# A twelfth weight slot laid over memory that the expert stage doesn't use

## The reference, cut to what matters

```
for layer in range(4):
    mixed = attention | hgrn2 | short_conv (x)          # 8, 10, 8 weight units of 2 MB
    x = layer_norm(alpha * x + mixed)
    logits = x @ w_group, x @ w_expert                  # group, then two experts in it
    h = silu(x @ w_gate[e]) * (x @ w_up[e]) * gate[e]   # e = 0..31, width 256
    x = layer_norm(alpha * x + sum_e h[e] @ w_down[e])
```

## Time and profile before

| what | us |
|---|---|
| median of 3 runs (1506.69 to 1510.03) | 1508.38 |
| the profiled execution | 1506.55 |
| its span, first to last instruction | 1504.4 |
| TensorE busy in it | 1342.5 |
| VectorE, ScalarE, GpSimd busy | 316.8, 312.0, 65.7 |
| bytes read from HBM | 478.22 MB |

### The profile page before, as it was taken

How to read it: one execution, slowest core, us unless ns; L and a number is a source line. 1 busy time by engine, 2 the same in 40 slices (tenths; PEclk the granted TensorE clock), 3 DMA queues, 4 the chain that set the end, 5 groups by cost and what they waited for, 6 DMA issues and landing times.

```text
span 1504.4 us, 18506 instructions
## 1 busy us (share of the span) xinstructions
PE 1342.5 (89%) x7798; PEld 760.4 (51%) x7798; DVE 316.8 (21%) x878; ACT 312.0 (21%) x765; POOL 65.7 (4%) x106
## 2 busy tenths in 40 slices
PE   8999988878999999888779999888789999888775
PEld 7866633332564776333327865332328675533321
DVE  0243311012100843101002133110021161301103
ACT  0242312112221422221112002211111251221110
POOL 2200000000000520000000000000001000000000
PEclk9999999999999999999999999999999999999998
DMA  9756499999733118999998936999997355699995
GB/s 322 290 196 248 162 426 430 426 428 425 301 133 146 58 30 366 415 426 429 426 429 337 388 121 219 431 425 430 426 426 323 113 224 223 251 429 426 428 425 221
DMA packets 35765, 480.60 MB, mean 319 GB/s; under 512 B 4304, under 2 KB 4624, under 8 KB 6368
## 3 DMA queue, kind: packets, MB, share of 16 engines
q1 hardware_dynamic: 34416, 476.79, 76.6%
q0 software_dynamic: 1120, 2.09, 0.7%
q10 hardware_dynamic: 144, 0.48, 0.1%
HBM read 478.22 MB, written 1.05 MB: 319 GB/s over the span
## 4 chain that ended last, share of the span: by engine, by line
PE 68%; DMA 23%; DVE 3%; ACT 3%; issue 1%; SPq 1%; POOL 0%; DVEq 0%; POOLq 0%
DMA ring<-in_units 17%; PE psum L742 15%; PE psum L1017 9%; PE psum L756 9%; PE psum L780 7%; PE psum L993 6%; DMA work<-in_units 5%; PE psum L1047 5%; PE psum L1055 5%; ACT work L1151 2%; PE psum L764 1%; PE psum L707 1%; PE psum L1109 1%; PE psum L820 1%; DVE work L1732 1%
## 5 line engine op out<-in xcount | busy, mean ns | idle before, releaser
L742 PE MATMUL psum<-xT,ring 128*128 128x256 f32 x1024 | 222.4, 379 | 1.4 <-DMA ring<-in_units 1.0
L742 PEld LDWEIGHTS psum<-xT,ring 128*128 128x128 f32 x1024 | 194.2, 190 | 28.8 <-DMA ring<-in_units 1.4
L1055 PE MATMUL psum<-work 128*128 128x512 f32 x256 | 128.7, 629 | 42.9 <-DVE work L1732 22.8
L1017 PE MATMUL psum<-ring,work 128*32 128x512 f32 x1200 | 143.2, 611 | 23.3 <-DMA ring<-in_units 23.3
L993 PE MATMUL psum<-work,x 128*128 128x128 f32 x1024 | 131.4, 283 | 35.1 <-ACT work L1151 35.0
L993 PEld LDWEIGHTS psum<-work,x 128*128 128x128 f32 x1024 | 120.9, 194 | 71.3 <-issue 68.0
L756 PE MATMUL psum<-ring,xT 128*128 128x512 f32 x320 | 138.6, 593 | 0.4 <-ACT xT L1151 0.4
L1151 ACT ACTIVATE work<-psum,affine_t 128x128 f32<-128x128 f32 x256 | 96.2, 456 | 123.9 <-PE psum L993 123.9
L1017 PE MATMUL psum<-work 128*32 128x512 f32 x848 | 104.2, 627 | 14.2 <-DMA work<-in_units 14.2
L1727 DVE TENSOR_TENSOR work<-work,psum 128x256 f32<-128x256 f32 x32 | 13.5, 421 | 484.9 <-ACT work L1318 484.9
L780 PE MATMUL psum<-ring,work 128*128 128x512 f32 x256 | 112.1, 593 | 0.9 <-DVE work L1406 0.9
(11 more groups left out here) (214 smaller groups left out, 1084.4 us busy)
## 6 DMA issues: line engine op xcount, KB each, us to landing
ring<-in_units SPq DMA_DIRECT2D x138, 2048.0 KB, 27.1
work<-in_units SPq DMA_DIRECT2D x83, 2048.0 KB, 26.3
ring<-in_units SPq DMA_DIRECT2D x6, 1024.0 KB, 45.8
ring<-in_units SPq DMA_DIRECT2D x4, 512.0 KB, 10.1
work<-in_units SPq DMA_DIRECT2D x2, 1024.0 KB, 45.0
x<-in_x SPq DMA_DIRECT2D x2, 512.0 KB, 4.1
out<-x SPq DMA_DIRECT2D x2, 512.0 KB, 2.7
work<-in_tables SPq DMA_DIRECT2D x1, 640.0 KB, 30.5
```

The costliest lines, as they stand in the source:

```text
L742: last = nc.tensor.matmul(bank(key, T, s * T), w[:, 2 * m + s, k, :], xT[:, k, :], start=(k == 0), stop=(k == KD - 1))
L1017: last = nc.tensor.matmul(psum[rows, 0, :].rearrange("p (t f) -> p t f", t=2), xw[:, k, rows], w[:, e, kk], start=(k == 0), stop=(k == KD ...
L1055: last = nc.tensor.matmul(psum[:, 4 + NH * c + h, :], hT[:, FC + c, :], y_sb[:, h * HB:(h + 1) * HB], start=False, stop=last_quad, skip_gr ...
```

## The change

The kernel gets a twelfth slot, `last`. It is laid over four things that are not read while the experts run: `xT` (2048 columns), the tables that only mixers, residual and rank use (`tri`, `ones`, `strict`, `alpha`, `causal`; 896 columns), the router weights (288 columns), and the first 864 columns of `work`. They become parts of one buffer, `memory`. The expert stage's own tiles (`scratch`) are packed into 4096 columns behind it; Silu's output goes straight into `h_sb`, and some tiles share places with `y_sb`.

The 48 expert units go through a cycle of 12. In each layer unit 11 is the first in slot `last`; it is loaded in two halves: the one over `xT` when the residual is through (`residual_made`), the other when the rank matmuls are. The down matmuls of unit 11 wait for both. The mixers wait for the reloaded tables ahead of their first use: the cumulative sum of the attention, the lower bounds of HGRN2, the residual of the convolution. Unit 47 uses the slot last. As the slot overwrites the tables and the router weights, SP loads the tables again in layers 1 to 3, behind the mixer's sixth unit and a wait for unit 47, and POOL loads the router weights after unit 47 of the layer before instead of after its logits. With 48 divisible by 12 the cycle ends where it began, so that the mixers' units find other ring slots: in layers 1 and 2 units 0 to 5 follow expert units 36, 37, 38, 39, 45, 46 (before: 42 to 47), in layer 3 units 40 to 44 and 46 (before: 37 to 41 and 43). The affine of the last normalisation, in e0, follows unit 42 (before: 39). `keep_busy` reads the identity four times over instead of 512 columns of tables.

```diff
-SLOTS = RING + EARLY
+SLOTS = RING + EARLY + 1
...
-                 2: [e1, e2, e3, e4] + r[2:] + [r[0], e0, r[1]]}[KINDS[l]]
+                 2: [e1, e2, e3, e4] + r[2:] + [r[0], e0, r[1]]}[KINDS[l]] + [last]
...
-EARLY_AT = 4688
+MIXER_TABLES = CONST_AT["iota"][0]
+SHARED = KD * T + MIXER_TABLES + KD * (NG + NE)
+MOE_SCRATCH = UNIT - SHARED
+EARLY_AT = 4960
...
-        const = sb("const", [P, CONST.shape[1]])
-        work = sb("work", [P, EARLY_AT + EARLY * UNIT])
+        const = sb("const", [P, CONST.shape[1] - MIXER_TABLES])
+        memory = sb("memory", [P, SHARED + EARLY_AT + EARLY * UNIT])
+        work = memory[:, SHARED:]
...
+        xT = region(memory, 0, [KD, T])
+        w_router = region(memory, KD * T + MIXER_TABLES, [KD, NG + NE])
...
+            if n == SLOTS - 1:
+                return memory[:, 0:UNIT]
...
-                    if KINDS[l] == 1 and m == RING - 1:
+                    if l and m == RING - 1:
 
                         sp.wait_ge(*moe_used(l - 1, NQ * QU - 1))
-                        sp.dma_start(tables, a["tables"]).then_inc(spans_in, 16)
+                        sp.dma_start(mixer_tables, a["const"][:, 0:MIXER_TABLES]).then_inc(tables_in, 16)
+                        if KINDS[l] == 1:
+                            sp.dma_start(tables, a["tables"]).then_inc(spans_in, 16)
...
+                if s == SLOTS - 1:
+                    sp.wait_ge(residual_made, l + 1)
+                    sp.dma_start(slot("moe", l, v)[:, 0:KD * T], a["units"][MOE_AT[l] + v][:, 0:KD * T]).then_inc(soon_in, 16)
+                    sp.wait_ge(*filled(("rank", l)))
+                    sp.dma_start(slot("moe", l, v)[:, KD * T:], a["units"][MOE_AT[l] + v][:, KD * T:]).then_inc(unit_in[s], 16)
...
-            sp.dma_start(const[:, first_const:], a["const"][:, first_const:]).then_inc(const_in, 16)
+            sp.dma_start(const[:], a["const"][:, MIXER_TABLES:]).then_inc(const_in, 16)
...
-                    pool.wait_ge(*filled(("logits", l - 1)))
+                    pool.wait_ge(*moe_used(l - 1, NQ * QU - 1))
                 pool.dma_start(w_router[:, :, 0:NG], ...)
...
-                    nc.tensor.matmul(psum[:, bank_no, :], ident, const[:, 0:HB], start=True, stop=True)
+                    nc.tensor.matmul(psum[:, bank_no, :], ident, ident.unsqueeze(1).to_broadcast([P, HB // P, P]), start=True, stop=True)
...
+                pe.wait_ge(tables_in, 16 * (l + 1))
...
+                    if sems is first and n % NQ * QU + GU + h == SLOTS - 1:
+                        pe.wait_ge(soon_in, 16 * (n // NQ + 1))
...
-                    residual([c])
+                    last = residual([c])
+                last.then_inc(residual_made, 1)
...
-                nc.scalar.activation(silu_g, psum[:, 0, 0:ED], ACT.Silu).then_inc(sems["silu_ready"], 1)
+                nc.scalar.activation(h_sb, psum[:, 0, 0:ED], ACT.Silu).then_inc(sems["silu_ready"], 1)
```

More of the change, by code:

```diff
@@ L70, in slot_plan @@
     order = list(range(RING))
-    e0, e1, e2, e3, e4 = range(RING, SLOTS)
+    e0, e1, e2, e3, e4, last = range(RING, SLOTS)
     def put(unit, slot):
@@ L287, in build @@
         x = sb("x", [P, TC, D])
-        xT = sb("xT", [P, KD, T])
         affine_t = sb("affine_t", [P, 2 * DEPTH, 2, KD])
-        const = sb("const", [P, CONST.shape[1]])
-        work = sb("work", [P, EARLY_AT + EARLY * UNIT])
+        const = sb("const", [P, CONST.shape[1] - MIXER_TABLES])
+        memory = sb("memory", [P, SHARED + EARLY_AT + EARLY * UNIT])
+        work = memory[:, SHARED:]
         extra = work[:, O_AT + TC * D:]
         small = sb("small", [P, 512])
-        w_router = sb("w_router", [P, KD, NG + NE])
         b_router = sb("b_router", [P, DEPTH, NG + NE])
         taps = sb("taps", [P, CW, KD])
-        most = sb("most", [P, DEPTH], I32)
         psum = ctx.enter_context(nc.psum_tensor("psum", [P, 8, HB], F32))
+        mixer_tables = memory[:, KD * T:KD * T + MIXER_TABLES]
         def table(name):
-            return const[:, CONST_AT[name][0]:CONST_AT[name][1]]
+            first, end = CONST_AT[name]
+            return mixer_tables[:, first:end] if end <= MIXER_TABLES else const[:, first - MIXER_TABLES:end - MIXER_TABLES]
         ident, ones, tri, strict = (table(n) for n in ("ident", "ones", "tri", "strict"))
@@ L325, in build @@
         lf_z = region(work, O_AT + 576, [TC, HEADS])
-        wf = region(work, 4544, [KD, HEADS])
-        bf = region(work, 4672, [HEADS])
+        wf = region(work, EARLY_AT - KD * HEADS, [KD, HEADS])
+        bf = region(small, 176, [HEADS])
         sm = region(extra, 0, [3, 384])
@@ L360, in build @@
         yT = region(work, 2048 + KD * PADT, [KD, T])
[L362 to L368, removed]
+        scratch = work[:, MOE_SCRATCH:EARLY_AT]
+        xw = region(scratch, 0, [KD, P])
+        sel = region(scratch, 1024, [2, TC, P])
+        selg = region(scratch, 1536, [2, TC, P])
+        h_sb = region(scratch, 2048, [ED])
+        hT = region(scratch, 2304, [FC + TC, P])
+        rank = region(scratch, 2816, [TC, NE])
+        gates = region(scratch, 2880, [TC, NE])
+        y_sb = region(scratch, 2944, [D])
+        picked, a1, a2, le, ranks = (region(scratch, 2944 + i * TC * NE, [TC, NE]) for i in range(5))
+        most = small[:, 192:192 + DEPTH].bitcast(I32)
         stats = region(small, 0, [TC, 2, 6])
@@ L396, in build @@
         lb_v = region(small, 320, [KD])
[L397 to L403, removed]
         const_in, b_in, w_r_in, wf_in, taps_in, lb_in, cum_in, norm_in = (
@@ L408, in build @@
         x_in = [sem(f"x_in{c}") for c in range(TC)]
-        affine_in, last_in, tables_in, spans_in = (sem(n) for n in ("affine_in", "last_in", "tables_in", "spans_in"))
+        affine_in, last_in, tables_in, spans_in, soon_in = (sem(n) for n in ("affine_in", "last_in", "tables_in", "spans_in", "soon_in"))
         unit_in = [sem(f"unit_in{s}") for s in range(SLOTS)]
@@ L418, in build @@
         ones_set = sem("ones_set")
+        residual_made = sem("residual_made")
         dve_step, act_step = sem("dve_step"), sem("act_step")
@@ L547, in experts @@
                     if v < SLOTS:
-                        slot_freed(l, v)
+                        first_load(l, v)
                     else:
                         sp.wait_ge(*moe_used(l, v - SLOTS))
-                    load(MOE_AT[l] + v, "moe", l, v)
+                    if v != SLOTS - 1:
+                        load(MOE_AT[l] + v, "moe", l, v)
             def load_quad(l, q, u, to, into):
@@ L763, in residual @@
                     for k in range(KD):
-                        nc.tensor.matmul(psum[:, 4 + NH * c + k // 4, k % 4 * P:(k % 4 + 1) * P], xT[:, k, c * P:(c + 1) * P], alpha_i,
-                                         start=(k % 4 == 0), stop=False, skip_group_check=True)
+                        last = nc.tensor.matmul(psum[:, 4 + NH * c + k // 4, k % 4 * P:(k % 4 + 1) * P], xT[:, k, c * P:(c + 1) * P], alpha_i,
+                                                start=(k % 4 == 0), stop=False, skip_group_check=True)
+                return last
             def output_projection(l, lhs, between=None):
@@ L807, in attention @@
                 pe.wait_ge(lf_ready, j + 1)
-                pe.wait_ge(tables_in, 16)
+                pe.wait_ge(tables_in, 16 * (l + 1))
                 nc.tensor.matmul(psum[0:HEADS, FILLS.bank[key], 0:T], lf[:, 0, :],
-                                 const[:, CONST_AT["tri"][0]:CONST_AT["ones"][1]], start=True, stop=False)
+                                 mixer_tables[:, CONST_AT["tri"][0]:CONST_AT["ones"][1]], start=True, stop=False)
                 nc.tensor.matmul(psum[0:HEADS, FILLS.bank[key], P:T], lf[:, 1, :], tri,
```

10 lines of the change are left out of this document (4 added, 6 removed).

## The result

The changed kernel takes **1485.67 us** in the median of four runs (1483.67 to 1487.88), against 1507.54 (1506.15 to 1510.03) for the kernel before beside it. The ratio is 0.9857, 95% interval 0.9841 to 0.9873: 21.9 us less, where 19.6 was forecast. One of the five executions of hold_half, a kernel of the experiments, took 7776 us for a reason that nothing traced shows, and is left out of its median.

The account below looks back on a forecast made before the run. The DMA queue was taken to bound the expert stages, TensorE the mixers. From the median 1508.38, minus 19.64 for one unit's transfer in four layers, plus 0.07 for SP's larger first load, gave 1488.8 us; range 1484 to 1494.

Parts of the forecast that it names:

- the term that carried it: Expert stages: unit 11 loads before the queue runs without a break, so each ends one transfer earlier, 19.64 us in all.
- The tight case, layer 1: Unit 11, queued behind unit 10, lands at about 601, just before the next load at 601.3; neither gap nor lateness.
- the additions: Added reloads, waits and moved loads cost nothing, except 0.07 us for SP's larger first load.
- The reloads: Tables in layers 1 to 3, in 4.1 us before use: nothing. Rival, waited for in each: 1501.9 us, chance 0.04.
- the router weights in a full queue: Moved behind the last expert unit, they take 3.3 us of the queue, hidden by the mixer units' cover.
- the waits of SP and POOL: SP's wait for unit 47 is just over; POOL's router issues take 7.8 us ahead of the convolution's memset: nothing.
- the affine loads: Last layer: waiting for unit 42 instead of 39, in at 1480.8, ahead of the last unit at 1486.7: nothing.
- the clock at the ends: Combine behind each layer's last landing, at the lower or upper clock: from -3.2 to +1.1 us, taken as 0.
- a mixer that grew: Sign of being wrong: any mixer longer than before; the mixers were expected to shift whole.
- The late half: Rival, layers 1 and 2: second half or all of unit 11 comes late, 1493.7 to 1498.6 us, chance 0.09.
- More than a unit: Rival: all tails behind the last landing as short as in layer 2, 1485.6 us, chance 0.07.
- the clock was held with the identity: Against rival: busy matmuls on the identity lose the clock, next mixer's first unit +13.9 us in three layers, 1530.5, chance 0.04.

Follow-up runs that it names:

- hold_half: Changed kernel with only the second half of unit 11 held back until unit 0 has been used; 1493.9 us.
- the dose experiment: Changed kernel with half a unit, one or two held until unit 0 is used; the four stages together grew by 9.5, 19.5 and 39.0 us.
- hold11: Changed kernel with twelve slots, but unit 11 loaded only when unit 0 has been used, as in the kernel before; 1504.22 us.
- tail_busy: Kernel before with one more busy matmul in each of three gaps of a layer's last quad; 1505.57 us beside 1508.79.
- after_again: The changed kernel run again unchanged, as the measure for the three that hold; 1485.71 us.
- the three that hold: hold_half, hold11, and the changed kernel with units 10 and 11 both held until unit 0 is used; 1493.9, 1504.22 and 1526.83 us.
- whole11: Changed kernel with unit 11 loaded in one piece when the rank matmuls are through, not in halves; 1486.39 us.
- busy_ident: Kernel before with one edit: the busy matmuls read the identity four times over instead of tables; 1506.30 us, ratio 0.9993.
- extras_only: Kernel before with busy matmuls on the identity, table reloads, their waits and the moved router weights, without a twelfth slot; 1506.93 us.

## Why the prediction was right

**Right to the tenth: the term that carried it.** 4 x 4.91 = 19.64 us were forecast; release to last landing gave 19.5, the dose experiment 19.5 for one unit in four layers. What made it right is the condition checked for each layer: that the queue was empty long enough ahead of the release. The tight case, layer 1, went nearly as worked out: its half is issued at 590.46 and the queue runs into the release at 597.13, and from release to last landing it gained 4.4 us of the 4.9.

**Right: the additions at nothing.** The reloads, the router weights in a full queue, the waits of SP and POOL, the affine loads. On POOL the second router issue waited 7.33 us in layer 2, more than the 6.01 of the earlier trace rows, and the memset began at once behind it at 788.58, 6.9 us ahead of the first drain at 795.50. The cover was 8 us by the forecast.

```profile
787.70 0.89 POOL L663 DMA_DIRECT2D memory<-in_moe_w_expert  x1 [7.33 <-issue]
788.58 0.14 POOL L699 MEMSET memory<- 128x16 f32 x1
```

The share that the small packets took of the full queue decided nothing, as they fell where units had a lead. The Trainium skill's page "DMA: Bandwidth & Descriptors", section "Specifications", with its 358 GB/s for a core, gives an estimate of 23.4 us for the four units; that it seems to come nearer to the 21.9 of the medians is chance, since the stages show 19.5 and 427 GB/s.

**Mis-sized: the clock at the ends.** It stood in the sum at 0, with a range from -3.2 to +1.1. The price of one tail was read from the combine's eight matmuls alone, 4.78 against 3.70; the down matmuls ahead of them slow down too, 1.64 against 1.07, so it is 1.64 from the last landing to the end. The three long tails all came out short in the profile (-4.9), as the short one stayed. I had taken them for chance; in twelve-slot kernels 30 of 32 are short. Over the medians this is the likeliest source of the 2.3 us beyond the forecast, and of the 3.1 us in hold11; tail_busy shows that removing these falls is worth 3.2 us in the kernel before. The sizes agree, but the proof in the changed kernel would need a tail that can be switched, and wasn't tried.

**Missed: falls of the clock inside the mixers.** The trace of before shows none behind the narrow matmuls, so I had no term for them. They cost the profiled execution 5.0 of the 5.7 us ahead of the experts (the other 0.7 lie at the start of layer 0), which fits that it is the slowest of its four. The prediction had named a mixer that grew as a sign of being wrong, and in this profile two did, by the clock and not by the change's own work. By them, less the shorter tails, the last landings came at 360.70 and 1469.53 us instead of 358.4 and 1467.1. That 5.7 us of loss and 4.9 us of gain nearly cancel in this execution is luck. The falls come in some executions: in or behind 7 of the 12 stretches in six profiles with twelve slots (after, after_again, the three that hold, whole11), none of 6 in before, busy_ident and extras_only, and 1 of 2 in tail_busy, which has the old slots too. That the change makes them likelier can't be told from so few.

**The rivals.** The late half can have cost at most the 0.5 us that are missing in layer 1. "More than a unit" was the nearest, with 1485.6 against 1485.67, and the profile shows what it named, all tails as in layer 2. That the number fits to 0.1 us is chance: the tails gave 4.9 us and not 3.2, and the mixers took some back. The reloads were not on the path, and the clock was held with the identity as well as with the tables (busy_ident), as the Trainium skill's page "TensorE: Matmul & The Clock Gate", section "Part 1: The HAM clock gate", has it, by which the clock follows how busy the array is.

## What to carry to other kernels

Where a stage is bound by the DMA queue, its end is the moment at which the queue starts to run without a break plus the bytes still to come. As long as the queue stays the last to end, another buffer is worth the bytes that it takes in before that moment, so look for an empty stretch of the queue ahead of the stage, and check for each layer that it is as long as the transfer. And read small differences against TensorE's clock first: a fall of the clock behind the last transfer costs time, and one while TensorE waits for the queue anyway doesn't.

## What the hardware showed that was not expected

- The granted clock fell to its lower level with TensorE busy throughout, towards the end of 32 matmuls of 16 columns in 4.24 us, for some 6 us, at a price of 3.3 us.
- The same gaps of TensorE (1.45, 0.47 and 1.4 us) stood ahead of a tail at the lower clock in the kernel before and ahead of one at the upper clock in hold_half.
- 32 more matmuls in each of two layers came with 5.4 us more in layers that don't contain them, 4.2 of it a stop of TensorE with no releaser behind the branch at the end of an expert stage.
- The stretches ahead of layers 1 and 2 are reproduced to 0.1 us between kernels (229.7 and 138.8) when neither happens, so that two profiles can be compared stretch by stretch far more exactly than two medians.
